# Last mixers: four projection halves placed behind the first heads' scores, norms of memory queries placed later and in other banks

## The reference

```python
h = rms_norm(x, norm_g[l])
q_a, k_a, v_a, q_h, f_h, i_h, q_m, z = split(h @ w_in[l])        # 20 panels of 256 columns
o_a = moba_attention(rope(rms_norm(q_a)), rope(rms_norm(k_a)), v_a)   # 8 heads of 64, causal
o_h = rms_norm(hgrn2_chunkwise(q_h, f_h, i_h))                   # 4 heads of 128
kv  = rms_norm(mem) @ w_mem_kv[l]                                # 256 memory rows
o_m = memory_attention(rms_norm(q_m), rms_norm(k_m), v_m)        # 4 heads of 128, not causal
x   = x + (concat(o_a, o_h, o_m) * silu(z)) @ w_out[l]
```

## Time and profile before

| | us |
|---|---|
| median of 3 runs | 1635.77 |
| the runs | 1633.10, 1636.43, 1635.77 |
| the profiled execution's own time | 1635.18 |
| its span in the profile | 1633.4 |
| TensorE matmul busy | 1550.5 (95%) |
| VectorE busy | 1152.6 (71%) |
| ScalarE busy | 758.9 (46%) |
| mean granted clock of TensorE | 0.975 |

### The profile page before, as it was taken

How to read it: one execution, slowest core, us unless ns; L and a number is a source line. 1 busy time by engine, 2 the same in 40 slices (tenths; PEclk the granted TensorE clock), 3 DMA queues, 4 the chain that set the end, 5 groups by cost and what they waited for, 6 DMA issues and landing times.

```text
span 1633.4 us, 26391 instructions
## 1 busy us (share of the span) xinstructions
PE 1550.5 (95%) x10678; PEld 1412.2 (86%) x10678; DVE 1152.6 (71%) x1363; ACT 758.9 (46%) x931; POOL 96.1 (6%) x66
## 2 busy tenths in 40 slices
PE   7999998998999999999997999999999899899988
PEld 6999998887899989999886899998999679799857
DVE  6867768636877777777676777777787665579654
ACT  5334446425533353333535533345646564555653
POOL 1000000010000000000000100002021001013000
PEclk9999999999999999999999999999999889999989
DMA  7555534204555545555431555554443215424202
GB/s 252 205 185 195 183 108 153 78 27 159 196 182 189 180 174 189 180 201 183 155 130 52 192 194 180 196 189 155 139 171 130 78 60 177 177 104 155 104 1 78
DMA packets 35869, 246.48 MB, mean 151 GB/s; under 512 B 3979, under 2 KB 5131, under 8 KB 6598
## 3 DMA queue, kind: packets, MB, share of 16 engines
q1 hardware_dynamic: 33552, 237.19, 40.6%
q0 software_dynamic: 1120, 6.96, 1.2%
q10 hardware_dynamic: 1110, 1.09, 0.2%
HBM read 244.18 MB, written 1.05 MB: 150 GB/s over the span
## 4 chain that ended last, share of the span: by engine, by line
PE 81%; DVE 11%; ACT 4%; issue 3%; DMA 1%; POOL 0%; ACTq 0%; DVEq 0%; POOLq 0%
PE ps L980 19%; PE ps L931 14%; PE ps L933 14%; PE ps L932 14%; PE ps L982 9%; PE ps L1153 4%; DVE act_two L1833 2%; DVE w_lo L1730 2%; PE ps L1297 1%; DVE x L1792 1%; ACT act_two L1493 1%; ACT w_hi L1400 1%; PE ps L1268 1%; ACT work L1624 1%; PE ps L1312 1%
## 5 line engine op out<-in xcount | busy, mean ns | idle before, releaser
L1400 ACT ACTIVATE w_hi<-raw 128x2048 fp32r<-128x2048 f32 x188 | 359.5, 1914 | 452.3 <-PE ps L982 262.9
L1730 DVE TENSOR_TENSOR w_lo<-raw,w_hi 128x2048 fp32r<-128x2048 f32 x188 | 438.0, 2335 | 156.8 <-ACT w_hi L1400 155.7
L980 PE MATMUL ps<-act_two,w_hi 128*128 128x512 f32 x1408 | 445.4, 398 | 8.1 <-DVE act_two L1833 3.7
L931 PE MATMUL ps<-act_two,w_hi 128*128 128x256 f32 x1120 | 329.6, 294 | 18.6 <-DVE act_two L1833 5.7
L982 PEld LDWEIGHTS ps<-act_two,w_lo 128*128 128x128 f32 x1408 | 265.8, 189 | 63.0
L932 PE MATMUL ps<-act_two,w_hi 128*128 128x256 f32 x1120 | 319.5, 285 | 0.0
L933 PE MATMUL ps<-act_two,w_lo 128*128 128x256 f32 x1120 | 319.2, 285 | 0.0
L982 PE MATMUL ps<-act_two,w_lo 128*128 128x256 f32 x1408 | 277.6, 279 | 0.0
L931 PEld LDWEIGHTS ps<-act_two,w_hi 128*128 128x128 f32 x1120 | 217.5, 194 | 25.6 <-issue 6.6
L980 PEld LDWEIGHTS ps<-act_two,w_hi 128*128 128x128 f32 x1408 | 215.5, 190 | 10.9 <-issue 4.4
L932 PEld LDWEIGHTS ps<-act_two,w_hi 128*128 128x128 f32 x1120 | 217.7, 194 | 3.5 <-issue 3.4
(11 more groups left out here) (269 smaller groups left out, 1875.8 us busy)
## 6 DMA issues: line engine op xcount, KB each, us to landing
raw<-panels SPq DMA_DIRECT2D x224, 1024.0 KB, 4.8
raw<-panels SPq DMA_DIRECT2D x8, 256.0 KB, 8.5
table<-tab POOLq DMA_DIRECT2D x1, 1472.0 KB, 8.8
table<-tab POOLq DMA_DIRECT2D x1, 1216.0 KB, 5.4
xn<-x_in ACTq DMA_DIRECT2D x4, 256.0 KB, 9.1
work<-mem_in POOLq DMA_DIRECT2D x1, 1024.0 KB, 9.0
xn<-mem_in POOLq DMA_DIRECT2D x1, 1024.0 KB, 5.1
out<-work POOLq DMA_DIRECT2D x4, 256.0 KB, 2.4
```

Of the source, the lines that this page charges most:

```text
L931: pe.matmul(o, l[0], r[0], start=start, stop=False, skip_group_check=shared)
L980: pe.matmul(grid(ps[:, bank + half], 2), w[half][0], act_two[:, slots[c]], start=c == 0, stop=False)
L1400: nc.scalar.activation(w_hi[:, s], raw[:, s], ACT.Copy).then_inc(panel_hi, 1)
L1730: tt(w_lo[:, s], raw[:, s], w_hi[:, s].bitcast(F32), ALU.subtract).then_inc(panel_lo, 1)
```

## The change

Four things change, in both last mixers. The last seven halves get other places: 16.1, 17.0, 17.1 stand behind rounds n+1, n+3, n+5 and the last four (18.0, 18.1, 19.0, 19.1) behind rounds h, h+1, h+1, h+2. The norms of the memory queries get a chain of their own that begins with cn_sq at h+5, so their sums come in rounds h+6 and h+7 in place of h and h+1, and write the banks of panels 18 and 19. `turn_back` moves from rounds h+2 to h+8 to rounds h+8 to h+14. New waits: cn_sum of sq waits for the evacuation of panel 18 or 19 (in place of ho's use), attend of the first MoBA head for ho's last use and the evacuation of panel 19, the first two turn_backs for cn_rstd of sq. `bank_of` is only moved up in the file.

```diff
 BESIDE_2 = [-13, -13, -12, -12, -11, -11, -10, -10, -9, -9, -8, -8, -7, -7, -6, -6, -5, -5, -4, -4, -3, -3, -2, -2,
-            -1, 0, 1, 2, 3, 4, 5, 6]
+            -1, 1, 3, 5, 7, 8, 8, 9]
...
-              [[]] * n + rounds(NORM_COLS, qk + [(f"ho{l}", 0), (f"ho{l}", 1), (f"sq{l}", 0), (f"sq{l}", 1)]),
+              [[]] * n + rounds(NORM_COLS, qk + [(f"ho{l}", 0), (f"ho{l}", 1)]),
+              [[]] * (h + 5) + rounds(NORM_COLS, [(f"sq{l}", 0), (f"sq{l}", 1)]),
...
-        chains += [[[]] * (h + 2) + sum(([[("pe", "turn_back", (b,)), ("act", "rows_back", (b,))], []] for b in range(PAIRS)), [])]
+        chains += [[[]] * (h + 8) + sum(([[("pe", "turn_back", (b,)), ("act", "rows_back", (b,))], []] for b in range(PAIRS)), [])]
...
-                norms[f"sq{l}", g] = (qm[:, s2], ones, 1 / P, sm(f"sq{l}"), qm[:, s2], None, None, 6 + g, evac(f"in2_{l}", 16 + g))
+                norms[f"sq{l}", g] = (qm[:, s2], ones, 1 / P, sm(f"sq{l}"), qm[:, s2], None, None, bank_of(f"in2_{l}", 18 + g), evac(f"in2_{l}", 16 + g))
...
             def turn_back(b):
 
                 if b < 2:
-                    pe.wait_ge(act_done, at("act", "evacuate", "in2_1", 18 + b))
+                    pe.wait_ge(act_done, at("act", "cn_rstd", ("sq1", b)))
...
                 if unit[0][:2] == "sq":
-                    pe.wait_ge(dve_done, at("dve", "cn_use", ("ho" + unit[0][2], unit[1])))
+                    pe.wait_ge(act_done, at("act", "evacuate", "in2_" + unit[0][2], 18 + unit[1]))
...
+                if unit[0].startswith("moba") and unit[1] == 0:
+                    pe.wait_ge(dve_done, at("dve", "cn_use", ("ho" + unit[0][4:], 1)))
+                    pe.wait_ge(act_done, at("act", "evacuate", "in2_" + unit[0][4:], 19))
                 if unit[0].startswith("matt") and unit[1] == 0:
```

More of the change, by code:

```diff
@@ L671, in build, with bank_of @@
         rope_index = {a[0]: i for i, a in enumerate(rope_list)}
+        def bank_of(name, k):
+            return 4 + (BASE[name] + k) % 2
         norms = {}
@@ L764, in build @@
                 dest[f"in2_{l}", 10 + k] = (blocks(z2, k), "cols", ACT.Copy)
-        def bank_of(name, k):
-            return 4 + (BASE[name] + k) % 2
         def sum_bank(tag):
```

## The result

The changed kernel is slower: median 1646.06 us of four runs (1643.06 to 1648.11) against 1635.95 of four runs of the kernel before (1633.10 to 1636.43), ratio 1.0058 [1.0043, 1.0073]. The profiled execution took 1645.68, 10.5 more than that of before. The prediction said 1640.0 with 1633.0 to 1644.0 around it: right in its sign, and the time is 2 us beyond the upper end.

A forecast was written before the change was run, and what follows sets the result against it. TensorE held 81% of the chain; full-clock attention rounds were bound by a VectorE-ScalarE-VectorE chain of 2.59 us. Timeline terms gave -0.4 and the clock +5.2, so +4.8 on the profiled 1635.18: 1640.0, 80% range 1633.0 to 1644.0.

The forecast's parts named there:

- M0 to T0: From mask_max start of the first MoBA head to that of the first memory head: 37.5 and 32.8 us, low clock included.
- T0 to T1: From mask_max start of the first memory head to the second's: as before, no cost forecast.
- M0: Start of mask_max of the first MoBA head, after the norm rounds: at 1283.8 instead of 1288.36, 4.5 us earlier.
- M1 to M2: Mask_max starts, second to third MoBA head: 4.9 us instead of 2.6, panel 190's split standing ahead of divide.
- case A: The forecast: clock falls at the first attend in both mixers, +4.8 us, 1640.0; chance 0.53.
- M6 to M7: Mask_max starts, seventh to eighth MoBA head: 4.78 us, with a memory query norm ahead of divide.
- Rival B: Clock holds at the first attend in one or both mixers: -0.4 to +2.2, 1634.8 to 1637.4; chance 0.27.
- Rival C: Clock holds and undisturbed attention rounds go by TensorE's 2.13 us: 3.7 gained, 1631.1; chance 0.12 with other unforeseen gains.
- The clock term of 2.6 a mixer: Around the first attend, a clock fall slows TensorE: 2.6 us a mixer, +5.2 for two.
- M2 to M3: Mask_max starts, third to fourth MoBA head: taken as a free round of 2.6 us.
- M5 to M6: Mask_max starts, sixth to seventh MoBA head: 9.96 us in the first mixer with mem1's statistics, 5.28 in the second.
- Rival D: Clock stays low through the memory heads too, three rounds a mixer: +6.6 on case A, 1646.6; chance 0.08.

The follow-up runs named there:

- evac_early: The changed kernel with the evacuation of panel 19 moved ahead of exp of head 3 on ScalarE; 1634.73 us, 0.9999 of the kernel before.
- warm: The changed kernel with five extra, never read matmuls on TensorE where it would idle at the first attend; 1640.34 us, 1.0025 of the kernel before.
- use_later: stats_late with memory queries' norms behind the attention's items and cn_use one round after its cn_rstd; 1620.90 us, 0.9918 (with three unused matmuls added 1617.10, 0.9886).
- norms_behind: evac_early with the memory queries' norm steps one round earlier and behind each round's attention items; 1637.08 us, 1.0002 of the kernel before.
- stats_late: evac_early with the row statistics and scaling of mem1 moved behind the first mixer's last head; 1631.23 us, 0.9967 of the kernel before.
- three_moves: evac_early with the moves of both norms_behind and stats_late; 1631.76 us, 0.9971 of the kernel before.
- halves_early: halves_only with the early evacuation of panel 19; 1625.72 us, 0.9943 (with mem1's statistics late as well 1622.74, 0.9929).
- norms_only: The changed kernel with the halves back at their old places, memory queries' norms and turn_backs still late; 1641.07 us, 1.0030 of the kernel before.
- halves_only: The kernel before with only the halves' new places and what they need, turn_backs from h+4, norms as before; 1635.93 us, ratio 0.9991.
- four_moves: three_moves with the last four halves behind rounds h, h, h+1, h+1; 1633.16 us, 0.9978 of the kernel before.

## Why the prediction was right in its sign and too low

**The sum, term by term.** Forecast +4.8, measured +10.5 in the profiles:

| | us |
|---|---|
| forecast | +4.8 |
| M0 to T0, first mixer, 39.22 for 37.5 | +1.7 |
| M0 to T0, second mixer, 34.56 for 32.8 | +1.8 |
| T0 to T1, second mixer, 4.15 for 2.90 | +1.25 |
| both M0 4.7 earlier instead of 4.5 | -0.4 |
| behind T1, second mixer, 0.2 for the 0.5 | -0.3 |
| between the mixers | +1.2 |
| ahead of the first mixer | +0.5 |
| measured | +10.5 |

**Right.** M0: 1284.10, less the 0.47 by which everything ahead of the stretch was late, is 1283.6 against 1283.8. That is no luck: VectorE has no idle time from the second cn_use (1264.12) to M0, with just the items that the prediction adds up. One reading on the way was wrong: it says that VectorE does less per norm round than TensorE's 3.73, while its own 2.96 and 1.23 make 4.19; TensorE's round also has a swap and is 4.6 (1262.96 to 1267.55 before the change). Nothing rests on it. M0 to M1 2.59, M1 to M2 5.29 and 4.87 for 4.9, the first attend behind the evacuation with 2.71 us idle for 2.9, the clock falling right behind it (case A, in both mixers), the statistics of mem1 in the chain (10.00 for 9.96), M6 to M7 4.86 for 4.78. Rival B is out: the clock did not hold at the first attend of either mixer. Rival C is out: the rounds without extra work at 2.4 GHz are 2.59 in evac_early, as forecast. The clock term of 2.6 a mixer was about right: 2.0 and 2.4, by warm. That four turn_backs leave no gap and that rows_back costs nothing fits the 0.2 behind T1.

**Mis-sized: M2 to M3.** The prediction counted TensorE's busy stretch up to 1293.7 and then took M2 to M3 as a free round of 2.6. By its own figures it was none: half 19.1 is 2.87 and stands ahead of turn_p of head 1 and scores of head 3, so that M3 can't come before TensorE is through. In the second mixer the half ran from 1562.08 to 1565.06 and M3 came at 1566.53, 3.17. In the first it was 4.24, since the clock also fell over half 18.0 (0.60 from 1279, then 0.83), which moved all of TensorE's work back. That fall was not foreseen. It came behind a new gap of 1.49 us, TensorE waiting for VectorE's act_two at 1278.43: the prediction says that TensorE has too little to bound anything there and didn't ask what the clock would make of it. evac_early, where the clock fell there in both mixers, has 4.24 in both; use_later, where it fell in neither, 3.18 and 3.19. Seven kernels have this gap and the same work behind it, and the clock fell over half 18.0 in 9 of their 14 mixers; none of the runs shows what decides. So 0.6 a mixer is TensorE's work and 1.0 that fall. M1 to M2 cost another 0.4 in the first mixer.

**Mis-sized: M5 to M6 in the second mixer**, 6.40 for 5.28. The prediction said that behind M5 the norms hide the low clock. They don't, because their own sum is TensorE's: it took from 1577.70 to 1579.57, 1.87 where it is 0.86 at full clock, and cn_rstd waited for it to 1579.82. With the clock up it is 5.33 (warm) and 5.32 (evac_early). What is hidden in a chain is only what is not itself a link of it.

**Failed: the memory heads of the second mixer.** The prediction put nothing there. Rival D had the clock low through all of them and got 0.08. It came in a smaller form: with 4.86 per round in M6 to M7, TensorE had 2.67 us of nothing (1587.72), the clock fell once more, and with turn_back at half clock between the heads T0 to T1 was 4.15 for 2.90. D's 1646.6 is next to the measured 1646.06 by luck: it comes from +6.6 over three rounds of both mixers, where the runs have +1.25 in one. warm, norms_behind, stats_late and three_moves have the same gap and the same price in the second mixer (4.05 to 4.24), and the last two even in the first, without turn_back (3.54, 3.61). The gap belongs to the norms' 4.86 round, and is a cost of moving the norms that the prediction lacked; other long rounds make it too, as the statistics did in halves_early. Whether the clock falls there is another matter. evac_early has the gap in its second mixer and kept 1.00, with T0 to T1 2.90:

```profile
1576.83 0.33 PE L1326 MATMUL ps<-const,work 128*128 128x128 f32 x1 [2.66 <-DVE work L2038]
...
1576.00:1579.00 3.00, 2.17 (x12) 1.46 (x12) 1.71 (x9) 1.34 (x5) 0.00 (x0) 1.00 0.00 0
```

**Not of the change: between the mixers.** From the first mixer's T0 to the last level_in of the second it is 201.6 us before and 202.8 after, 1.2 more, though no item differs there. Windows of before and then of after, in the norm ahead of the next layer:

```profile
1440.00:1445.00 5.00, 2.39 (x12) 2.40 (x13) 3.35 (x4) 4.72 (x6) 0.00 (x0) 0.78 0.00 0
1445.00:1450.00 5.00, 5.00 (x39) 5.00 (x39) 4.97 (x7) 3.13 (x4) 0.00 (x0) 0.88 0.32 98
```

```profile
1445.00:1450.00 5.00, 2.50 (x11) 2.50 (x12) 3.34 (x4) 4.72 (x6) 0.00 (x0) 0.69 0.00 0
1450.00:1455.00 5.00, 5.00 (x31) 5.00 (x30) 4.97 (x7) 3.03 (x4) 0.00 (x0) 0.63 0.42 118
```

The clock came back later. The same distance is 202.7 in warm and 201.6 in evac_early, again with the same items. Ahead of the first mixer the scatter is larger: the last level_in there stands anywhere from 1251.7 to 1256.8 in the 14 profiled executions, and nothing in front of it differs. So a microsecond or two either way is chance; a forecast from one profile can't have it, a range should. Without these 1.7 us the profiled execution would have been at the upper edge of the range. The range had 4 us above the forecast and needed 6; more than two thirds of the miss are the terms above.

**Where the loss comes from**, by what it gave to take one thing away after the other: the evacuation of panel 19 behind exp of head 3, 9.7 us by the ratios (some 5.4 of it the clock), the statistics of mem1 inside the norms' chain 5.2, VectorE's wait for cn_rstd ahead of divide 8.0. These are more than the loss of 9.5, since against them stand the gains that the prediction names, which use_later keeps; and the statistics cost 2.3 before the change too (M6 to M7 4.86 against 2.60).

**The turn_backs.** The prediction weighed a rule of the Trainium skill, "TensorE: Matmul & The Clock Gate", Part 4: PE-mode transpose, by which transposes don't count as busy for the clock in the way that matmuls do, against rows that suggested they had helped it up. Before the change the second mixer, with x transposes in those rounds, had its clock up at 1575, and the first, without, was still low at 1315, half a stretch further in the earlier trace rows. norms_only has them from h+8 on, and its second mixer is at 0.50 in the window from 1575. halves_only has them from h+4 on:

```profile
1314.00:1317.00 3.00, 3.00 (x11) 1.62 (x10) 2.11 (x8) 1.88 (x8) 0.00 (x0) 0.50 0.01 3
1575.00:1578.00 3.00, 3.00 (x19) 2.04 (x18) 1.43 (x9) 1.78 (x6) 0.00 (x0) 1.00 0.00 0
```

There too it was up at 1575 in the mixer with transposes, 8.5 us behind its gap at 1566.5, and still low at 1314 in the one without, 14 behind its gap at 1300.0. How long the clock stayed low in the rounds of the MoBA heads, by the record of the granted clock, first mixer / second, in whole us: before 27 / 14 and halves_only 17 / 7, with transposes there in the second mixer only; norms_only 17 / 17, four_moves 10 / 14 and after 10 / 10, with none in either. By that rule the second mixer would gain nothing over the first; it did in the two kernels that have the transposes, and in none of the others. The statistics of mem1 also set the first mixer apart, but they do so in norms_only and after as well. No run had the transposes' place as its only difference, so this is a hint and not shown.

## What to carry to other kernels

When work is moved behind a consumer's wait, look at the queue of every engine that the released piece passes: here an evacuation stood behind an exp it had nothing to do with, and moving that one item was worth more than the whole change. An in-order engine that needs another's result should get it one round after it was made; putting the consumer merely later within the same round changed nothing here. Before a start in one profile is compared with a start in another, subtract what was late ahead of the stretch: norms_only looks as if it had gained nothing at M0, and had gained 1.6 us. Ask of every gap that an edit opens between thin matmuls what comes behind it at half clock, and of every term "hidden" whether it is a link of the chain that hides it.

## What the runs showed of the hardware

The clock falls behind shorter gaps than I had thought: in four_moves one of 1.38 us, between scores and an attend, was followed by the fall from 1.00 to 0.50 in both mixers. And the same gap needn't do the same twice. The 1.49 us ahead of scores of head 0 was followed by 0.60 in the first mixer of after and by no fall in the second, nor in use_later; the 2.7 us ahead of head 5's turn_p came with a fall in the second mixer of five kernels and with none in that of evac_early. The Trainium skill says something near this of the rise at a kernel's start, which comes after a different number of matmuls from run to run ("TensorE: Matmul & The Clock Gate", Part 1: The HAM clock gate); no run here shows that start. On the other side, rounds without a gap of TensorE can hold 2.4 GHz with scores over 64 rows, transposes and attends alone: use_later has 1.00 at 1303 to 1306 with 3.00 us busy of 3. The same kind of rounds, once low, stayed at 0.50 for 27 us in the first mixer of before. That is how shortening VectorE's and ScalarE's chain can pay twice, when the gap it closes would have come with a fall: stats_late has the gap of 2.67 us, the fall and T0 to T1 of 3.54 and 4.21, use_later has neither the gap nor the fall, and 2.90.
